# Four starting places modulo 128 bytes for the weight ring and the two halves of x, in a fused two-block fp32 kernel

## What is computed

```python
def first_block(x, w_in, ...):              # twice
    proj = x @ w_in[l]                       # 1024 x 8200
    y_ret = retention(...) @ w_proj_ret[l]   # 1024 x 1024
    y_ml  = mlstm(...)     @ w_proj_mlstm[l] # 1024 x 1024
    mix = (gate_a * y_ret + gate_b * y_ml) @ w_out[l]
    x = layer_norm(ALPHA * x + mix)
    gu = x @ w_gate_up[l]                    # 1024 x 5632
    x = layer_norm(ALPHA * x + (silu(gu[..., :FF]) * gu[..., FF:]) @ w_down[l])

def second_block(x, ...):                    # twice, then a final norm
    hn = rms_norm(x)
    proj = hn @ w_in_2[l]                    # 1024 x 3584
    y = concat(dilated_attention, rg_lru, stick_breaking_attention) * silu(gates)
    x = x + y @ w_out_2[l]
```

## Time and profile before

| | us |
|---|---|
| median of 3 runs | 1225.78 |
| lowest and highest | 1225.24 and 1227.17 |
| the profiled execution | 1227.07 |
| its span, first to last instruction | 1225.3 |
| PE busy, 7560 matmuls | 1201.7 |
| weight loads busy, 7560 | 1068.6 |
| DVE busy | 739.7 |
| ACT busy | 570.5 |
| POOL busy | 25.9 |

### The profile page before, as it was taken

How to read it: one execution, slowest core, us unless ns; L and a number is a source line. 1 busy time by engine, 2 the same in 40 slices (tenths; PEclk the granted TensorE clock), 3 DMA queues, 4 the chain that set the end, 5 groups by cost and what they waited for, 6 DMA issues and landing times.

```text
span 1225.3 us, 18032 instructions
## 1 busy us (share of the span) xinstructions
PE 1201.7 (98%) x7560; PEld 1068.6 (87%) x7560; DVE 739.7 (60%) x990; ACT 570.5 (47%) x656; POOL 25.9 (2%) x35
## 2 busy tenths in 40 slices
PE   6999999999999999999999999999999999999997
PEld 5978998997999988888998997999987788878895
DVE  4866556667655556566665668655456655765565
ACT  5454445442544434454445533444344455846563
POOL 0000000001000000000000001000000000000000
PEclk9999999999999999999999999999999999999999
DMA  8744545556656463744545556856554553446320
GB/s 290 259 166 145 171 146 184 186 182 203 219 188 191 150 210 114 256 147 137 172 140 172 174 188 186 271 176 190 186 193 138 187 174 104 138 154 215 104 70 34
DMA packets 129823, 211.71 MB, mean 173 GB/s; under 512 B 6480, under 2 KB 52560, under 8 KB 129616
## 3 DMA queue, kind: packets, MB, share of 16 engines
q1 hardware_dynamic: 126944, 203.23, 50.3%
q0 software_dynamic: 1744, 6.29, 1.8%
q10 hardware_dynamic: 1056, 1.05, 0.3%
HBM read 209.50 MB, written 1.05 MB: 172 GB/s over the span
## 4 chain that ended last, share of the span: by engine, by line
PE 93%; DVE 3%; ACT 3%; issue 1%; DMA 0%; POOL 0%; DVEq 0%; POOLq 0%; ACTq 0%
PE ps L428 89%; PE ps L617 1%; ACT wh L890 1%; PE ps L751 1%; PE ps L652 1%; DMA hml<-in_xT 0%; PE ps L600 0%; PE ps L559 0%; ACT sg L1053 0%; ACT xh L926 0%; DVE sg L1585 0%; DVE wl L1311 0%; PE ps L734 0%; PE ps L624 0%; DVE yl L1774 0%
## 5 line engine op out<-in xcount | busy, mean ns | idle before, releaser
L1311 DVE TENSOR_TENSOR wl<-raw,wh 128x2048 fp32r<-128x2048 f32 (+2 forms) x195 | 428.9, 2206 | 193.6 <-ACT wh L890 193.0
L890 ACT ACTIVATE wh<-raw 128x2048 fp32r<-128x2048 f32 (+2 forms) x195 | 363.4, 1870 | 191.0 <-PE ps L428 178.3
L428 PE MATMUL ps<-xh,wh 128*128 128x256 f32 (+1 forms) x1200 | 344.8, 287 | 0.0
L428 PE MATMUL ps<-xl,wh 128*128 128x256 f32 (+1 forms) x1200 | 339.3, 283 | 0.0
L428 PE MATMUL ps<-xh,wl 128*128 128x256 f32 (+1 forms) x1200 | 339.2, 283 | 0.0
L428 PEld LDWEIGHTS ps<-xh,wh 128*128 128x128 f32 (+1 forms) x1200 | 228.2, 190 | 4.7 <-issue 3.4
L428 PEld LDWEIGHTS ps<-xl,wh 128*128 128x128 f32 (+1 forms) x1200 | 228.4, 190 | 0.9
L428 PEld LDWEIGHTS ps<-xh,wl 128*128 128x128 f32 (+1 forms) x1200 | 228.3, 190 | 0.4
L428 PE MATMUL ps<-wh,xh 128*128 128x512 f32 (+1 forms) x512 | 205.3, 401 | 13.8 <-DVE wl L1311 11.6
L428 PE MATMUL ps<-wh,xl 128*128 128x512 f32 (+1 forms) x512 | 197.8, 386 | 0.0
L428 PE MATMUL ps<-wl,xh 128*128 128x512 f32 (+1 forms) x512 | 197.7, 386 | 0.0
(11 more groups left out here) (243 smaller groups left out, 1382.5 us busy)
## 6 DMA issues: line engine op xcount, KB each, us to landing
raw<-in_w_in SPq DMA_DIRECT2D x91, 1024.0 KB, 5.1
raw<-in_w_gate_up SPq DMA_DIRECT2D x88, 512.0 KB, 5.0
raw<-in_w_down SPq DMA_DIRECT2D x20, 1024.0 KB, 5.1
raw<-in_w_out SPq DMA_DIRECT2D x16, 1024.0 KB, 5.0
raw<-in_w_proj_ret SPq DMA_DIRECT2D x8, 1024.0 KB, 5.0
raw<-in_w_proj_mlstm SPq DMA_DIRECT2D x8, 1024.0 KB, 5.0
rows<-in_ln_g POOLq DMA_DIRECT2D x4, 512.0 KB, 4.1
rows<-in_ln_b POOLq DMA_DIRECT2D x4, 512.0 KB, 5.8
```

The lines of the kernel that those rows point to most:

```text
L428: return pe.matmul(o, a, b, start=start, stop=False, skip_group_check=True)
L890: act.activation(wh[u % RING][:, 0:m], raw[u % RAW][:, 0:m], ACT.Copy).then_inc(s_hi, 1)
L1311: dve.tensor_tensor(wl[u % RING][:, a:nk * n], raw[u % RAW][:, a:nk * n], f32(wh[u % RING][:, a:nk * n]), ALU.subtract).then_inc(s_lo, 1 i ...
```

## The change

Four tensors that nothing reads or writes are allocated ahead of the four wh buffers, four ahead of the wl buffers, one ahead of xh and one ahead of xl. No instruction is added, removed or moved.

```diff
         raw = [sb(f"raw{i}", [P, KU * 512]) for i in range(RAW)]
-        wh = [sb(f"wh{i}", [P, KU * 512], F32R) for i in range(RING)]
-        wl = [sb(f"wl{i}", [P, KU * 512], F32R) for i in range(RING)]
+        wh, wl = [], []
+        for i, gap in enumerate((24, 8, 8, 8)):
+            sb(f"gap_wh{i}", [P, gap])
+            wh.append(sb(f"wh{i}", [P, KU * 512], F32R))
+        for i, gap in enumerate((24, 8, 8, 8)):
+            sb(f"gap_wl{i}", [P, gap])
+            wl.append(sb(f"wl{i}", [P, KU * 512], F32R))
         X = sb("X", [P, 2, D])
+        sb("gap_xh", [P, 24])
         xh = sb("xh", [P, 8, S], F32R)
+        sb("gap_xl", [P, 16])
         xl = sb("xl", [P, 8, S], F32R)
```

## The result

The changed kernel takes 1228.89 us (median of 11 runs, 1228.31 to 1231.54), the kernel before 1225.78 us (11 runs). The ratio is 1.0029, with a 95% interval of 1.0019 to 1.0038: slower by 0.3%. I had forecast 1190. The time lies inside the stated range, but it moved the other way. The range had been drawn as far as 1237 to take in the slower rival, so that it holds this time says nothing for the forecast's own steps. The two profiled executions, at the same granted clock (0.997), have spans 4.0 us apart where the medians are 3.1 apart.

A forecast was written before the change was run, and what follows sets the result against it. PE's pace of starting matmuls was taken to bound the kernel. Gains of 37.0, 1.9 and 1.3 us summed to 40.2, cut by a tenth to 36: from 1227.07 to 1191, forecast 1190 us, range 1170 to 1237.

The forecast's parts named there:

- the slower rival: Equal starts are a good state for 512 columns; leaving them costs 12.5 us in all, giving 1238; chance 0.17.
- What bounds the kernel: Whole kernel: it goes as fast as PE starts matmuls; VectorE and ScalarE have slack in gate_up.
- The tenth that I took off for side work: VectorE and ScalarE chains beside PE come out as its cover shortens by 8%: the 40.2 us gain becomes 36.
- The base: Every fp32r matmul: 6.7 ns from moving starts 32 bytes off a multiple of 64; removal saves 28.8 and 7.8 us.
- the second reading: Rival: the base is a fixed cost of each fp32r matmul, only collisions change, about -4 us, 1222; chance 0.17.
- The split by the gate step: Gate step, 8 stationary columns, 113.3 ns: overhead 6.7 of 13.3 ns needs no real weight load, the rest is collision.
- if the step still goes at 113.3: Sign in the gate step with 8 stationary columns: if its pace stays there, the base is fixed and the forecast wrong.
- The collision: Moving stream against next weight load, by start distance: mean 3.9 ns with 256 columns, 10 ns with 512 after the change.
- The period of four units: Sign in gate_up: starts 106.7 to 113.3 ns apart instead of 120.0, differing from unit to unit in fours.
- Nothing happens: Rival: the 13.3 ns are one fixed cost whatever the starts, and the time stays 1226; chance 0.06.
- The collisions go altogether: Rival: collisions vanish except at distance 0, and the base too; 108.3 and 218.3 ns, time 1156; chance 0.08.

The follow-up runs named there:

- at 1203 us: On the kernel with xh and xl at 224, om and or also moved to 224, hd and y kept with the ring: 1203.3 us, ratio 0.9818.
- x both at 224: Against the kernel before, two gaps start xh and xl both at 224 modulo 256, counting the ring's place as 32: 1209.14 us, ratio 0.9865.
- the map: Separate kernel without the model: PE alone runs groups of 48 fp32r matmuls at start distances 0 to 480 bytes; 256 columns at distance 0 took 120.0 ns.
- The two kernels of PE alone: The map, and a second kernel without the model varying leading matmuls, widths and types; at distance 64 the second showed 117.8 or 113.3 ns.
- x at 96: Against the kernel before, gaps start xh and xl both at 96 with the ring at 32: 1221.29 us, ratio 0.9964.

## Why the prediction was wrong

**What bounds the kernel: right.** PE's starts set the time, as its 98% of busy time and 93% of the chain had it. In every run the table's paces, times their counts, give the change of the median within 1.5 us, and VectorE and ScalarE took over no place on the path: at 1203 us they have 2% of it each, PE 93%. The tenth that I took off for side work didn't show where there was a gain to lose it from: by the table x both at 224 should save 3552 x 5.4 - 1440 x 2.3 ns = 15.9 us, and it saved 16.6.

**The base: wrong, and it decided the sign.** I had explained 6.7 ns of every fp32r matmul by a start 32 bytes off a multiple of 64, on the ground that it is exactly the time of 64 bytes. With every start on such a multiple the paces of all forms but one stayed, and that one got slower. The term was 36.6 of 40.2 us and measured 0. What stood for it was one number that fitted; all moving operands of the kernel before had the same offset from 64, so its trace could not tell a cost of the offset from a fixed cost. I gave the second reading 0.17. That no row could tell them apart was itself in the text, and the chances didn't follow it. In all runs no fp32r group with 256 columns went below 113.3 ns, and none with 512 below 226.7, so at least that overhead of 6.7 ns stays in fp32r at all placements tried. The run with everything moved by 96 bytes speaks for the fixed cost: there the offset was free (1226.33 us against 1225.30).

**The split by the gate step: wrong.** I had read its 113.3 ns as the pace without a collision, because only 8 columns are loaded. After the change the same step goes at 116.5 ns instead of 114.3, so with a load of 8 columns the places count as well. In the map's groups with 8 stationary columns the pace was 113.3 to 120.0 ns, and at each distance the two repetitions differed (at 128, 113.3 and 120.0), so 113.3 was no sign of a missing collision. As a sign it failed too: I had said that the base is fixed if the step still goes at 113.3; the base is fixed, and it doesn't. The run with everything moved by 96 bytes is what decided.

**The collision: right in that the distance counts, with the wrong period and the wrong sizes.** That the distance between the moving start and the weight load counts, and in both directions, is what the map and the model's runs show; the alternating groups show that it isn't all. The period of four units that I had named as a sign is there too, at 117.3 to 119.5 ns and not at 106.7 to 113.3. But I took the distance modulo 128. Modulo 256 the ring's four places, 32 apart, give the moving xh distances 128, 96, 64, 32 from wh, and the moving xl 0, 224, 192, 160 from wl. With 256 columns I had said 3.9 ns over the base and it is 118.2 - 113.3 = 4.9. With 512 I had said 10 and it is 232.7 - 220.0 = 12.7, because 32, 96 and everything from 128 up cost 12.4 to 14.3 ns and not the 10 that I had put between two rows. With the base fixed, my sizes gave -4 us; the paces measured in the changed kernel, times their counts, are +4.5, and the medians 3.1 apart.

**The rival that was slower: half right.** It put the loss where it is: equal starts are the best of the map's distances for 512 columns (226.7 ns), and leaving them cost x, hd and y 10.6 us over 2160 matmuls, 4.9 ns each, against the 5.0 that it assumed. Its other half, 120 ns with 256 columns at every distance, fell: 120.0 is the highest of the map's values for that form on its grid of 32 bytes, and leaving it gave back 5.9 us. So the time ended between that rival (1238) and the one with the fixed base (1222).

**Nothing happens: the nearest number, by luck.** 1226 is 3 us off, nearer than any other case, because 5.9 us less and 10.4 us more nearly cancel; both were to be zero. Its premise, one fixed cost of 13.3 ns whatever the starts, fell: in the map the distance between the moving and the stationary start alone moved the pace from 113.3 to 120.0 and from 226.7 to 234.3 ns, in fp32r. Other engines have no part in that: with VectorE, ScalarE and DMA idle the paces are those of the model (120.0 and 226.7 ns at equal places). Nor is all of the 13.3 ns a cost of every matmul: in the same kind of stream bf16 went at 109.2 and 215.8 ns, fp32r at 113.3 and 226.7 at best.

**The collisions go altogether: wrong.** It had 108.3 and 218.3 ns. No group of the map went below 113.3 and 226.7 at any place.

**What stays open.** What gives the pace its period of 256 bytes, and why the best distance differs between 256 and 512 columns, no run settles. At distances 64 and 192 with 256 columns there are two steady states, 113.3 and 117.8 ns, and what ran ahead of a group chooses between them. The two kernels of PE alone agree on it where they do the same, and two such paces at one distance are what yr0 and yr1 show. But at 192 the same number of small matmuls led to 113.3 the first time and to 117.8 the second, yr1 changed over when everything moved by 96 bytes, and with x at 96 the two layers' gate_up differ: I have no rule to choose it. In gate_up with x at 224 both layers ran at 113.3, in each of the two kernels built so. Each placement was profiled once, so how often a kernel takes which pace isn't shown. What else than the load beside a matmul acts on its pace when starts alternate is open too.

## What to carry to other kernels

Where fp32r matmuls are limited by their own pace, the starting places of the moving and the stationary tensor modulo 256 bytes are worth a trial: here two unused gaps gave 1.35%, six edits of placement 1.8%. Measure the map once on PE alone, by distance and by width, and place each pair of tensors by it, then read the paces in the kernel, since two of the distances have two paces. Spreading the places evenly gives about the mean of the map (on x 118.2 and 232.7 ns, where the mean over the map's eight distances is 118.1 and 231.9), which is no gain where one form sat at its best. And a term of a sum that rests on one fitting number, with every row of the trace at the same value of the supposed cause, should get no more chance than its rival.

## What the runs showed of the hardware that I had not expected

- fp32r matmuls with 128 stationary columns started 113.3 to 120.0 ns apart with 256 moving columns and 226.7 to 234.3 with 512, by the distance of the two starts modulo 256 bytes in steps of 32, with no other engine at work and a granted clock of 0.999. bf16 (109.2 and 215.8 ns) and fp32 (215.8 ns with 256 columns) showed none of it at the distances tried.
- Distances that are no multiple of 32 aren't better: at 4 bytes 123.3 and 237 ns, the worst of all; at 8 and 16 bytes 116.7 with 256 columns, 233.3 and 231.6 with 512. At 240 bytes with 512 columns one group went at 226.7 and its repetition at 236.7; at 496, the same distance modulo 256, both went at 236.7.
- The same sequence of matmuls can settle into either of two paces 4% apart (113.3 or 117.8 ns) and keeps it: with x at 96 more than 800 matmuls of gate_up went at 117.8 in one layer and at 113.3 in the other.
